# Query projections of a product-key layer in three one-pass products, with the remainders of the weights made on GpSimd

## What is computed

```
q = (xb @ w_q).reshape(PEER_BLOCK, PEER_HEADS, 2, PEER_DQ // 2)      # 8 heads, 2 halves of 128
s = jnp.einsum("nhcd,hckd->nhck", q, sub_keys)                       # 128 keys a half
v1, i1 = lax.top_k(s[:, :, 0], 16); v2, i2 = lax.top_k(s[:, :, 1], 16)
top_s, pos = lax.top_k(v1[..., :, None] + v2[..., None, :], 16)      # 256 candidates
gate = softmax(top_s); act = gelu(xb . u_tab[eidx]); out = (gate * act) @ v_tab[eidx]
```

## Time and profile before

| | us |
|---|---|
| median of 3 executions | 3032.56 (3030.48 to 3035.35) |
| profiled execution | 3031.55 |
| its span, first to last instruction | 3029.70 |
| busy TensorE / VectorE / GpSimd / ScalarE | 2821.5 / 2578.8 / 1592.9 / 911.0 |
| first score block read by VectorE | at 605.91 |
| first one-hot instruction on VectorE | at 1022.29 |

### The profile page before, as it was taken

The page is one execution under the profiler, slowest core; times in us unless marked ns, Lnnn a source line. Parts: engine busy times, 40 slices in busy tenths (PEclk is TensorE's granted clock), DMA queues, the critical chain, the costliest instruction groups (busy, mean ns, idle before and its releaser), DMA issues.

```text
span 3029.7 us, 48280 instructions
## 1 busy us (share of the span) xinstructions
PE 2821.5 (93%) x16748; PEld 2372.2 (78%) x16748; DVE 2578.8 (85%) x5656; ACT 911.0 (30%) x1793; POOL 1592.9 (53%) x1215
## 2 busy tenths in 40 slices
PE   7999799999998577599999999999999999999996
PEld 3566358677776476599999999999999999999995
DVE  6481355379999999599999999999999999999998
ACT  3213230244444699212111121111111211112123
POOL 0000000035757000567777777777777777777774
PEclk9999899999998799799999999999999999999998
DMA  5012631599998566999999999999999999999996
GB/s 213 20 42 44 224 130 63 180 336 333 339 326 318 194 184 193 352 376 405 400 409 410 411 409 400 411 410 411 411 399 405 409 408 401 409 404 406 408 411 250
DMA packets 326527, 959.32 MB, mean 317 GB/s; under 512 B 37248, under 2 KB 119216, under 8 KB 313088
## 3 DMA queue, kind: packets, MB, share of 16 engines
q0 software_dynamic: 147456, 536.94, 44.8%
q1 hardware_dynamic: 166160, 416.65, 37.5%
q10 hardware_dynamic: 12816, 4.60, 0.7%
HBM read 841.10 MB, written 116.85 MB: 316 GB/s over the span
## 4 chain that ended last, share of the span: by engine, by line
PE 30%; DVE 27%; issue 14%; DMA 13%; POOL 10%; ACT 4%; DVEq 0%; ACTq 0%; SPq 0%; POOLq 0%
POOL ring L633 10%; DMA ring<-in_vt,arena 10%; DVE h_rows L2051 6%; PE ps L912 6%; DVE ring L2034 5%; PE ps L771 4%; PE ps L1018 3%; PE ps L895 2%; PE ps L721 2%; ACT arena L1350 2%; DVE u_lo L1494 2%; PE ps L869 2%; PE ps L878 2%; DVE y_sum L1494 2%; DVE arena L1494 2%
## 5 line engine op out<-in xcount | busy, mean ns | idle before, releaser
L633 POOL DMA_INDIRECT ring<-u_table,arena x512 | 687.6, 1343 | 389.0 <-PE ps L992 154.8
L633 POOL DMA_INDIRECT ring<-in_vt,arena x512 | 648.5, 1267 | 204.7 <-issue 133.6
L1018 PE MATMUL ps<-h_hi,u_hi 128*128 128x320 f32 (+1 forms) x2048 | 649.8, 317 | 44.6 <-DVE u_lo L1494 42.4
L2034 DVE SCALAR_TENSOR_TENSOR ring<-ring,h_rows 128x1024 f32<-128x1024 f32 x512 | 622.8, 1216 | 45.5 <-DMA ring<-u_table,arena 38.2
L1018 PE MATMUL ps<-h_lo,u_hi 128*128 128x320 f32 (+1 forms) x2048 | 606.7, 296 | 0.0
L1018 PE MATMUL ps<-h_hi,u_lo 128*128 128x320 f32 (+1 forms) x2048 | 606.6, 296 | 0.0
L1035 PE MATMUL ps<-w,v_rows 128*128 128x320 f32 (+1 forms) x2048 | 579.5, 405 | 0.0
L2051 DVE SCALAR_TENSOR_TENSOR h_rows<-ring,s5c,h_rows 128x1024 f32<-128x1024 f32 x381 | 495.0, 1299 | 24.3 <-DMA ring<-in_vt,arena 23.7
L1018 PEld LDWEIGHTS ps<-h_hi,u_hi 128*128 128x128 f32 x2048 | 388.7, 190 | 64.3 <-DVE u_lo L1494 33.0
L1035 PEld LDWEIGHTS ps<-w,v_rows 128*128 128x128 f32 x2048 | 358.3, 189 | 54.4
L1018 PEld LDWEIGHTS ps<-h_lo,u_hi 128*128 128x128 f32 x2048 | 388.8, 190 | 5.3
(11 more groups left out here) (282 smaller groups left out, 4344.7 us busy)
## 6 DMA issues: line engine op xcount, KB each, us to landing
u_turn<-in_ut SPq DMA_DIRECT2D x128, 512.0 KB, 5.3
u_table<-u_turn SPq DMA_DIRECT2D x128, 512.0 KB, 4.0
v_rows<-in_vt SPq DMA_DIRECT2D x64, 1024.0 KB, 9.7
u_raw<-in_ut SPq DMA_DIRECT2D x126, 512.0 KB, 6.7
c_raw<-coef_dram SPq DMA_DIRECT2D x64, 576.0 KB, 8.8
coef_dram<-arena SPq DMA_DIRECT2D x8, 4096.0 KB, 15.9
arena<-in_w_ada SPq DMA_DIRECT2D x24, 1024.0 KB, 7.5
arena<-in_xp SPq DMA_DIRECT2D x2, 4096.0 KB, 12.8
```

The lines of the kernel that those rows point to most:

```text
L633: nc.gpsimd.indirect_dma_start(out=slot(n), out_offset=None, in_=table, in_offset=bass.IndirectOffsetOnAxis(ap=uvi[:, at:at + 1], axis=0)) ...
L1018: last = mm(ps[b0 + j if first else j % 2][:, 0:width], w[a][:, k, :], ph[b][:, k, 64 * c0:64 * c0 + width], start=k == 0 and n == 0, stop ...
L2034: V.scalar_tensor_tensor(out=row, in0=row, scalar=1.0, in1=h_rows[:, bass.ds(1024 * tile_of[0], 1024)], op0=ALU.mult, op1=ALU.mult, accum_ ...
```

## The change

h2 is split into a rounded part and a remainder when it leaves PSUM, for the first 512 rows (`s_hi`, `s_lo`) and for the other 576 (`h_hi`, `h_lo`), by two passes of ScalarE or VectorE over each bank and a subtraction on VectorE. The query weights are split too: ScalarE copies the rounded part of each half-head's weights (`wq_first`, into `wq_hi`), and GpSimd makes the remainder in place (`wq_rest`, into `wq_lo`). A query chunk is then 24 one-pass matmuls; the chunks are now 512, 320 and 256 rows (`QCH`). A head has 15 table tiles instead of 14, in 6 buffers instead of 7. For head 0 the three chunks of half 0 and key_scores(0, 0) come ahead of all but one of its tiles.

GpSimd makes the remainders for heads 0 and 1 before its loop; those for head h+2 are made inside decode(h), the first half after its part for half 0, the second after it has signalled `decoded`. TensorE's query(h, c, 0) waits for `wq_lo_ready`. The late `h_hi` and `h_lo` copies after the heads are gone, and the rows of h2 for the sparse part are turned from both parts.

```diff
-TURN = (23296, 24320, 25344, 4608, 5632, 6656, 7680)
-NTURN, TPH = 7, 14
+TURN = (22784, 23808, 24832, 25856, 47744, 48768)
+NTURN, TPH = 6, 15
+QCH = ((0, 512), (512, 320), (832, 256))
...
-            def decode(h):
+            def decode(h, between):
...
+                    if c == 0 and between:
+                        between(0)
                 last.then_inc(s("decoded"), 1)
                 pool.wait_ge(s("decoded"), h + 1)
+                if between:
+                    between(1)
...
+            def wq_rest(h, hb, c):
+                o = 2048 * hb + 1024 * c
+                pool.wait_ge(s("wq_hi_ready"), 2 * h + c + 1)
+                nc.gpsimd.tensor_tensor(wq_lo[:, o:o + 1024], seg(wq_buf, o, 1024),
+                                        wq_hi[:, 1024 * c:1024 * c + 1024].bitcast(F32), ALU.subtract).then_inc(
+                    s("wq_lo_ready"), 1)
+
+            for h in range(2):
+                for c in range(2):
+                    wq_rest(h, h, c)
+            with pool.Fori(0, HEADS // 2 - 1) as i:
+                for hb in range(2):
+                    decode(2 * i + hb, lambda c: wq_rest(2 * i + (hb + 2), hb, c))
+            decode(HEADS - 2, None)
...
+            parts = ((0, 0), (0, 1), (1, 0))
...
+            def query(hd, hb, c, q, of=0, tiles=(), first=False):
+
+                w = [v[:, o:o + 1024].rearrange("p (k n) -> p k n", k=8)
+                     for v, o in ((wq_hi, 1024 * c), (wq_lo, 2048 * hb + 1024 * c))]
+                if q == 0:
+                    pe.wait_ge(s("wq_lo_ready"), 2 * hd + c + 1)
...
                 for k in range(8):
-                    last = mm(ps[q][:, 0:width], w[:, k, :], h2[:, k, P * k0:P * k0 + width],
-                              start=k == 0, stop=k == 7)
+                    for n, (a, b) in enumerate(parts):
+                        last = mm(ps[q][:, 0:width], w[a][:, k, :], parted[q > 0][b][:, k, c0:c0 + width],
+                                  start=k == 0 and n == 0, stop=k == 7 and n == 2)
...
+            def head(hd, hb, i, last=False):
+                r0 = TPH * hb
+
+                query(hd, hb, 0, 1, i, (r0, r0 + 1))
+                query(hd, hb, 0, 2, i, (r0 + 2, r0 + 3))
+                query(hd, hb, 1, 0, i, (r0 + 4, r0 + 5))
+                turn_tile(i, r0 + 6)
+                key_scores(hd, 0)
+                query(hd, hb, 1, 1, i, (r0 + 7, r0 + 8))
+                query(hd, hb, 1, 2, i, (r0 + 9, r0 + 10))
+                if not last:
+                    query(hd + 1, 1 - hb, 0, 0, i, (r0 + 11, r0 + 12))
+                    turn_tile(i, r0 + 13)
+                    turn_tile(i, r0 + 14)
                 key_scores(hd, 1)
...
+            for q in range(3):
+                query(0, 0, 0, q, first=True)
+            stage_emptied(pe, "h2T")
+            pe.wait_ge(s("keys_in"), 16)
+            turn_tile(0, 0, True)
+            key_scores(0, 0, True)
+            for q in range(3):
+                query(0, 0, 1, q, 0, (2 * q + 1, 2 * q + 2))
...
+            def wq_first(h, i, hb, c, first=False):
+                act.wait_ge(s(f"wq_in{hb}"), 16 * i + 16)
+                if not first:
+                    act.wait_ge(s("q_full"), 6 * h + 3 * c - 3)
+                nc.scalar.copy(wq_hi[:, 1024 * c:1024 * c + 1024], seg(wq_buf, 2048 * hb + 1024 * c, 1024)).then_inc(
+                    s("wq_hi_ready"), 1)
...
                 table_tile(i, r0 + 6)
                 s_moves(0)
+                if not last:
+                    wq_first(h + 1, i + hb, 1 - hb, 0)
                 moves(1, 1, 7)
                 moves(1, 2, 9)
-                if not first:
-                    softmax_exp(h - 1)
+                softmax_exp(h - 1)
                 if not last:
                     for r in range(11, TPH):
-                        table_tile(h, r)
+                        table_tile(i, r0 + r)
+                    wq_first(h + 1, i + hb, 1 - hb, 1)
                 s_moves(1)
...
-            dve.wait_ge(s("h_split"), 1)
-            for b in range(3, NTURN):
-                table_stored(dve, b)
-            tt(h_lo[:, :].rearrange("p (k n) -> p k n", k=8),
-               seg(h2_buf, 0, 8704).rearrange("p (k n) -> p k n", k=8)[:, :, NSC:NT],
-               h_hi[:, :].rearrange("p (k n) -> p k n", k=8).bitcast(F32), ALU.subtract).then_inc(s("h_split"), 1)
-            dve.wait_ge(s("h_split"), 2)
             dve.wait_ge(s("picksT_moved"), 6)
```

More of the change, by code:

```diff
@@ L337, in modulated, with h2_piece @@
                                                 ALU.mult, ALU.add).then_inc(emptied["dve"], 1)
+        parted = [[v[:, :].rearrange("p (k n) -> p k n", k=8) for v in pair] for pair in ((s_hi, s_lo), (h_hi, h_lo))]
+        h2 = seg(h2_buf, 0, 4608).rearrange("p (k n) -> p k n", k=8)
+        def h2_piece(part, q, j):
+            return parted[q > 0][part][:, j, :] if q == 0 else parted[1][part][:, j, 512 * (q - 1):ND if q > 1 else 512]
         @block.sync
@@ L446, in turn_table @@
                     b = (r + 4) % NTURN
-                    if not (first and r < 3):
-                        sp.wait_ge(s(f"table_out{b}"), 64 * i + 16 * ((r - 3) // NTURN) + 16)
+                    if not (first and r < NTURN - 4):
+                        sp.wait_ge(s(f"table_out{b}"), 80 * i + 16 * ((r + 4 - NTURN) // NTURN) + 16)
                     load(turn_buf[b][:, :], A["ut"][bass.ds(2 * TPH * i + r + 4, 1)].rearrange("t p n -> (t p) n"),
@@ L916, in query @@
                     if tiles and k % 2:
-                        turn_half(of, tiles[k // 4], k // 2 % 2, first)
+                        turn_half(of, tiles[k // 4], k // 2 % 2)
             def key_scores(hd, c, first=False):
@@ L949, in _ @@
+            turn_tile(0, 7)
+            key_scores(0, 1)
+            query(1, 1, 0, 0, 0, (8, 9))
+            for r in range(10, TPH):
+                turn_tile(0, r)
             with pe.Fori(0, HEADS // 2 - 1) as i:
-                head(2 * i + 1, 1, i, i + 1)
-                head(2 * i + 2, 0, i + 1, i + 1)
-            head(HEADS - 1, 1, HEADS // 2 - 1, None)
+                head(2 * i + 1, 1, i)
+                head(2 * i + 2, 0, i + 1)
+            head(HEADS - 1, 1, HEADS // 2 - 1, last=True)
@@ L1295, in s_moves @@
                     nc.scalar.copy(ar(SB + 1152 * c + 1024, P, DSEQ), ps[5][0:DSEQ, 0:P]).then_inc(s("s_moved"), 1)
+                if first:
+                    for q in range(3):
+                        q_move(0, q)
+                    table_tile(0, 0)
+                    s_moves(0)
+                    wq_first(1, 0, 1, 0)
+                    for q in range(3):
+                        moves(1, q, 2 * q + 1)
+                    wq_first(1, 0, 1, 1)
+                    table_tile(0, 7)
+                    s_moves(1)
+                    for r in range(8, TPH):
+                        table_tile(0, r)
+                    return
                 q_move(0, 0)
@@ L1860, in _, with h2_pieces @@
             dve.wait_ge(s("a2_ready"), 1)
-            modulated(dve, "dve", "h2T", h2_buf, a2, 24)
+            def h2_pieces(q, j):
+                b = filled(dve, "h2T", 8 * q + j)
+                if q == 1:
+                    dve.wait_ge(s("h_split"), j + 1)
+                for out in (h2[:, j, 0:512], h2_piece(0, q, j)):
+                    last = ts(out, b[:, :], a2[:, j, 0:1], mcol[:, 24 + j, 0:1], ALU.mult, ALU.add)
+                done(last)
+            for q in range(2):
+                for j in range(8):
+                    if j in (0, 2):
+                        h2_pieces(q, 2 * j)
+                    stage_emptied(dve, "h2T", 8 * q + j + 1)
+                    tt(h2_piece(1, q, j), h2[:, j, 0:512], h2_piece(0, q, j).bitcast(F32), ALU.subtract).then_inc(
+                        s("h_split"), 1)
             stage_emptied(dve, "h2T")
+            tt(parted[1][1][:, :, 512:ND], h2[:, :, 512:ND], parted[1][0][:, :, 512:ND].bitcast(F32),
+               ALU.subtract).then_inc(s("h_split"), 1)
             dve.wait_ge(s("x1_out"), 48)
@@ L1983, in _ @@
             assert got == NLINK, got
-            table_stored(dve, 2)
+            for b in (2, 3):
+                table_stored(dve, b)
             i1, i2 = ar(IALL, NSC), ar(IALL + 1152, NSC)
```

150 lines of the change are left out of this document (82 added, 68 removed).

## The result

The changed kernel takes 3103.4 us (median of four runs, 3100.18 to 3106.39), the kernel before 3032.05 in the same series: a ratio of 1.0227 [1.0214, 1.0239]. The forecast was 3077 us, at most 3092. It is slower as forecast, by 71 us in place of 44. The profiled execution is the one of 3100.18 us, with a span of 3098.4; the span before was 3029.7. The 68.7 us between the two spans lie in two stages, and I take them in order of time.

The account below looks back on a forecast made before the run. VectorE was taken to set the heads' rhythm at 48.5 us; the new wait makes five periods of 58.5 after P(1) at 707, +48.3, less 4.1 at the stage's end: 3077 us, range 3056 to 3092.

Parts of the forecast that it names:

- The loop and its terms: Heads: P(h), GpSimd, TensorE, ScalarE, VectorE, P(h+1) form a closed loop; period 58.5 us against 48.5.
- P + 14.1: P(h) is decode(h)'s start, VectorE done with head h's positions; GpSimd's first subtraction releases TensorE's query 14.1 us later.
- the ring: The closed loop of hand-overs from one P(h) to the next, through GpSimd's subtraction; forecast 58.5 us a head.
- The clock's term: After about 13 us idle in each head, TensorE restarts at a lower clock and loses 2.3 us.
- The end of the stage: After the heads, VectorE no longer makes the 4.95 us split `h_lo`; 4.1 us are gained.
- the long ends: Upper bounds of the loop's terms, summed in the prediction to a period of 60.4 us.
- The start: Heads 0 and 1: P(0) at 645.8, 12 us earlier; P(1) at 707, allowed 702 to 712, early start spent.
- both gates off: Neither GpSimd subtraction holds TensorE's queries; the prediction had the first as the loop's wait, the second as harmless.
- The later stages move by that.: After the heads, all later stages shift by the heads' net delay, +44.2 us, and change no further.
- The rival of the lock: GpSimd's two subtractions a head block VectorE's two-input instructions, 26 us in all: 3103 us; 3%.
- The clock rival: TensorE's clock stays low through query, tiles and key scores, 5 to 6 us a period: 3092 to 3095; 4%.
- The first rival: The new wait is not on the path and VectorE stays the bound at 48.5 us: 3027 us; 5%.
- the second gate: TensorE's wait for the second half of `wq_lo`, ready about P + 40; delays nothing VectorE needs before P + 63.

Follow-up runs that it names:

- The sixth kernel: The changed kernel with one more 128x1024 GpSimd operation ahead of the subtraction between decode's halves: 3112.4 us, 1.0242.
- the seventh: The changed kernel with VectorE's code shifted by 16 instructions and second-half key scores ahead of the next head's query: 3061.3 us, 1.0072.
- fifth kernel: The changed kernel, VectorE's code shifted by 16 instructions, first GpSimd subtraction ahead of decode, second inside decode's second half: 3046.9 us, 1.0026.
- the eighth: The fifth kernel with second-half key scores also ahead of the next head's query and tiles 11 to 14: 3044.2 us, 1.0024.
- the ninth: The fifth kernel with ScalarE's exponentials of head 0 made earlier, ahead of the second query's copies in head 1: 3042.6 us, 1.0033.

## Why the prediction was right and wrong

**The loop and its terms were right.** Per head, forecast and measured at head 4: release at P + 14.1, measured 900.99 - 887.04 = 13.95; query, four half-tiles, clock and tiles 13 and 14, 7.3 + 2.3 + 2.7 = 12.3, measured to the key scores 12.06; key scores to VectorE 3.65, measured 3.62; VectorE's block to P 28.4, measured 28.44. Sum 58.5, measured 58.07, and 58.10 in the mean from P(1) to P(6). The sixth kernel shows that the GpSimd term is on the path, the seventh that the order on TensorE closes the ring. The clock's term can be read off against the second half-query, which runs at a clock of 1.00: the query and its four half-tiles take 9.41 us behind the gap (900.99 to 909.96 + 0.44) and 7.77 there, of which 0.3 are a pause ahead of the first half-tile. So the clock cost 1.6 to 2.0 us, forecast 2.3. The end of the stage gained 4.05 for 4.1. Two sums of the working are slightly off: 707 + 5 x 58.5 is 999.5, not 999.6, and the long ends that it names add up to 59.9 us, not 60.4, which would put its upper end at 3089.

**The start was 5.6 us short.** P(0) came at 647.26 for 645.8, P(1) at 712.62 for 707, just outside 702 to 712. I had let TensorE alone set P(1), with the scores at 675. They start at 680.11, and VectorE is held to the same moment by something that the working doesn't have: it waits 23.5 us for the exponentials of head 0 (to 670.69) and gets through its first block at 684.4. With both gates off P(1) is at 716.14 (fifth kernel); the eighth (scores early, 719.89) and the ninth (exponentials early, 717.40) don't bring it forward, so either one holds P(1) alone. That "the early start is spent" was right.

**The step that failed is "The later stages move by that."** From P(6) on they don't. Of the 26.7 us between the forecast (3076.75 before rounding) and the median, 20.4 are the sparse stage, 3.6 lie ahead of the first one-hot (P(6) 1003.12 for 999.6: the start's 5.6 less five periods that were 0.4 shorter), 0.5 in the one-hots, and 2.2 are that the profiled execution lay 3.2 below the median, not 1.0. 18.1 of the 20.4 us are VectorE's holes behind jumps back, by the instruction queue a fetching of code: they go with 16 idle instructions in the changed kernel (16.0 us between the profiled spans, 19 between the medians) and 17.1 us of them come with 28 in the kernel before. The 2 to 4 us that are left have no cause shown; four executions of one kernel scatter by 5 to 6. The change lengthened VectorE's code ahead of that loop and had no other part in it. No row of the trace of before has a hole of this kind, so neither end of the range had it. With the code shifted, the changed kernel takes 3084.6 us, inside the range.

**The rivals.** The rival of the lock gave 3103 us, the time that was measured, but that is chance and not its mechanism: none of the stretched instructions lies on the changed kernel's ring, whose VectorE term is the 28.44. With both gates off the stretch is there, 1 us a head on the candidate sums. The clock rival did not come. The first rival, the wait that isn't on the path, set 3027; the fifth kernel is that case made real, and 3047 is what it gives, 8.6 above the kernel before measured beside it. It lacked the second ring, the second gate being called harmless ("delays nothing that VectorE needs before P + 63"): true beside the first ring, and the longest one as soon as the first was gone.

**Where the change's gain went.** By the prediction's terms TensorE saves 43 us of matmuls over the stage, and none of it is on the path: VectorE's 48.5 us a head bound the heads before and, with both gates off, bind them at 49.5.

## What to carry to other kernels

- Work moved to an engine that an earlier hand-over of the same loop releases can close a ring. Add up the ring, every ring that passes through the moved piece and also those over two heads, and compare each with the present period; taking the longest away shows only the next one.
- An idle time of VectorE named "issue" right behind a loop's jump back, with more packets on the instruction queue, points to code fetching. Its cost belongs to where the loop lies, so shift the code by some instructions before blaming, or praising, a change.
- Two kernels that differ by more than a few instructions on an engine with loops can differ by 1.3% for that alone.

## What the runs showed of the hardware

- A jump back on VectorE cost two idle times of 4.1 to 5.0 us in the third sparse loop, in kernels whose three other loops of the same body jump back free; in the heads' loop of the changed kernel they were 4.4 to 5.4 and 1.3 to 1.6 us. 28 instructions that only wait, all put ahead of the first loop, cost the old kernel 40 us.
- The number of packets on the instruction queue (52 to 54, or 88) told the state of a kernel without its timeline.
- VectorE's MAX8 and FIND_INDEX8 instructions kept their lengths beside GpSimd (272 and 281 ns with decode beside most of them, 271 and 279 before); only the two-input instructions were stretched. From P(1) to P(6) the ten a head took 853 ns in the mean before and 380 in the changed kernel, where VectorE reaches its candidate sums after decode is over.
